# Last pair of experts: both first matrices fetched and multiplied ahead of both second matrices, and the last half matrix fetched in three parts

## The reference

```python
def reference(x, ...):                       # x (1, 256, 1024), all float32
    h = rmsnorm(x, mix_norm)
    z = h @ w_in                             # split: pool, q, k, v, indexer, gates
    y_pool = pool_mixer(z_pool) @ w_branch_pool
    y_attn = dsa_attention(q, k, v, ...) @ w_branch_attn
    x = x + (gates[0] * y_pool + gates[1] * y_attn) @ w_out
    h2 = rmsnorm(x, ffn_norm)
    x = x + moe(h2, ...)
    return rmsnorm(x, final_norm)

def moe(h, ...):                             # 256 tokens, 32 experts, 4 of them per token
    logits = h @ w_router + b_router
    top_vals, top_idx = top_k(logits, 4)
    gates = softmax(top_vals)
    combine = sum over the 4 of one_hot(top_idx) * gates
    for e in range(32):
        gu = h @ w1[e] + b1[e]               # w1[e] is 1024 x 2048: 8 MB
        g_ = min(gu[:, :1024], 7)
        u_ = clip(gu[:, 1024:], -7, 7)
        act = g_ * sigmoid(1.702 * g_) * (u_ + 1)
        out += combine[:, e] * (act @ w2[e] + b2[e])   # w2[e] is 1024 x 1024: 4 MB
```

## Time and profile before

| | |
|---|---|
| median of 3 runs | 1103.54 us (1103.14 to 1104.28) |
| the profiled execution | 1103.12 us |
| its span in the trace | 1101.2 us, so 1.9 us lie around it |
| PE busy | 1021.2 us, 93% |
| DVE, ACT busy | 28%, 20% |
| mean granted TensorE clock | 0.986 |
| moved | 438.34 MB, mean 398 GB/s |

### The profile page before, as it was taken

How to read it: one execution, slowest core, us unless ns; L and a number is a source line. 1 busy time by engine, 2 the same in 40 slices (tenths; PEclk the granted TensorE clock), 3 DMA queues, 4 the chain that set the end, 5 groups by cost and what they waited for, 6 DMA issues and landing times.

```text
span 1101.2 us, 12231 instructions
## 1 busy us (share of the span) xinstructions
PE 1021.2 (93%) x4994; PEld 503.4 (46%) x4994; DVE 303.5 (28%) x689; ACT 218.6 (20%) x373; POOL 18.3 (2%) x26
## 2 busy tenths in 40 slices
PE   5999999999999999998998989898989898999896
PEld 5987776434343434343434343434333343434342
DVE  5866576221212121212121211212121111121212
ACT  6456644111111111111111101011101111111112
POOL 1100020000000000000000000000000000000000
PEclk9999999999999999999999999999999999999999
DMA  8784469999999999999999999999999999999994
GB/s 321 290 329 148 153 258 417 426 430 430 431 431 428 436 432 430 437 430 432 432 438 431 432 432 438 431 432 432 438 431 432 432 438 431 432 427 430 432 428 183
DMA packets 25635, 438.34 MB, mean 398 GB/s; under 512 B 3016, under 2 KB 3200, under 8 KB 5120
## 3 DMA queue, kind: packets, MB, share of 16 engines
q1 hardware_dynamic: 24432, 432.84, 92.5%
q0 software_dynamic: 1168, 5.01, 1.2%
HBM read 436.78 MB, written 2.11 MB: 399 GB/s over the span
## 4 chain that ended last, share of the span: by engine, by line
PE 67%; DMA 27%; DVE 2%; issue 1%; ACT 1%; SPq 0%; DVEq 0%; ACTq 0%
PE bank L1424 28%; DMA quad<-in_w 21%; PE bank L1473 14%; DMA place<-in_w 6%; PE bank L1085 6%; PE bank L1086 5%; PE bank L1087 5%; PE bank L1329 3%; PE bank L1286 1%; PE bank L1454 1%; DMA cst<-in_consts 1%; PE bank L1397 1%; PE bank L1379 1%; PE bank L1433 0%; DVE wl L712 0%
## 5 line engine op out<-in xcount | busy, mean ns | idle before, releaser
L1424 PE MATMUL bank<-quad,r 128*64 128x512 f32 x1280 | 294.4, 618 | 22.2 <-DMA quad<-in_w 22.2
L1424 PEld LDWEIGHTS bank<-quad,r 128*64 128x64 f32 x1280 | 98.3, 142 | 205.9 <-issue 201.5
L1424 PE MATMUL bank<-place,r 128*64 128x512 f32 x704 | 154.6, 595 | 4.8 <-DMA place<-in_w 3.7
L1473 PE MATMUL bank<-quad,r 128*64 128x512 f32 x640 | 141.7, 595 | 11.2 <-issue 7.8
L996 DVE TENSOR_SCALAR r<-bank 128x512 f32<-128x512 f32 x32 | 22.1, 692 | 404.9 <-PE bank L1424 391.9
L1018 DVE TENSOR_TENSOR ysl<-bank,ysh 64x512 fp32r<-64x512 f32 x62 | 42.7, 688 | 291.1 <-ACT ysh L662 290.1
L643 ACT ACTIVATE r<-r 128x512 f32<-128x512 f32 x32 | 20.2, 632 | 471.0 <-DVE r L996 471.0
L1424 PEld LDWEIGHTS bank<-place,r 128*64 128x64 f32 x704 | 49.4, 137 | 102.4 <-issue 94.9
L1473 PEld LDWEIGHTS bank<-quad,r 128*64 128x64 f32 x640 | 51.1, 137 | 90.5 <-issue 90.5
L1473 PE MATMUL bank<-place,r 128*64 128x512 f32 x352 | 78.0, 595 | 6.0 <-issue 5.3
L662 ACT ACTIVATE ysh<-bank 64x512 fp32r<-64x512 f32 x62 | 36.6, 591 | 225.6 <-PE bank L1473 224.8
(11 more groups left out here) (214 smaller groups left out, 815.4 us busy)
## 6 DMA issues: line engine op xcount, KB each, us to landing
quad<-in_w SPq DMA_DIRECT2D x60, 4096.0 KB, 29.3
place<-in_w SPq DMA_DIRECT2D x69, 2048.0 KB, 17.7
ring<-in_w_front SPq DMA_DIRECT2D x24, 1024.0 KB, 4.9
place<-in_w SPq DMA_DIRECT2D x2, 1024.0 KB, 34.7
place<-in_w_last SPq DMA_DIRECT2D x1, 2048.0 KB, 36.0
place<-in_w_last SPq DMA_DIRECT2D x2, 1024.0 KB, 34.7
ring<-in_w_idx SPq DMA_DIRECT2D x2, 768.0 KB, 6.8
xs<-in_x SPq DMA_DIRECT2D x2, 512.0 KB, 8.2
```

Of the source, the lines that this page charges most:

```text
L1424: ins = mm(bk[part, :], xgT[i // 2 % 2][:, k, own], w[:, c1:c1 + HALF], start=False, stop=k == KD - 1)
L1473: ins = mm(YT[part, :], a_k, w[:, kk, c1:c1 + HALF], start=k == 0, stop=k == KD - 1)
```

## The change

- The transfers of the last pair are issued in another order: chunks 12 to 15 w1 of 30, 16 to 19 w1 of 31, 20 and 21 w2 of 30, 22 and 23 w2 of 31. The places and the waits before each issue are the same. Chunk 21 is one transfer instead of two; chunk 23 is three (1 MB, 0.5 MB, 0.5 MB) instead of two.
- PE follows: w1 of 30, scatter of the former pair, gate transposes, transposes of `act` of 30 (now in bank `GATHER`, copied to a new tile `actT_even`), both biases, w1 of 31, w2 of 30 (in `YT`), transposes of `act` of 31, `scatter_even`, w2 of 31 (summed in `UA` and `GATHER`), with the scatter of the first half (`scatter_last(0)`) placed after half of the matmuls of the second.
- The gather that stood in expert 30 for an expert that doesn't exist is moved into the branch for experts with more than 64 tokens.
- ACT and DVE do their work for the last pair in that order.

The three functions `last_pair` below are, in this order, those of ACT, DVE and PE.

```diff
+            last_order = [(NE - 4, range(CHUNKS)), (NE - 3, range(CHUNKS)), (NE - 2, range(4)), (NE - 1, range(4)),
+                          (NE - 2, range(4, CHUNKS)), (NE - 1, range(4, CHUNKS))]
+            for c, (e, j) in enumerate((e, j) for e, js in last_order for j in js):
+                i = halves[c % (2 * QUADS)][0]
                 former = 2 * (c - 2 * QUADS + 1) if c >= 2 * QUADS else 4 * (c // 2 - QUADS + 1)
                 sp.wait_ge(chunks_used, (NE - GROUP) * STEPS + former)
+                if (e, j) == (NE - 1, CHUNKS - 2):
+                    sp.dma_start(place[i], w2_last[0, :, :]).then_inc(chunk_loaded[i], 16)
+                elif (e, j) == (NE - 1, CHUNKS - 1):
+                    for lo_col, hi_col, loaded in ((0, SLOT, chunk_loaded[i]), (SLOT, SLOT + PIECE, tail_loaded[0]),
+                                                   (SLOT + PIECE, CHUNK, tail_loaded[1])):
+                        sp.dma_start(place[i][:, lo_col:hi_col], w2_last[1, :, lo_col:hi_col]).then_inc(loaded, 16)
...
+            def last_pair():
+                u = NE - 2
+                sigmoid(u)
...
+                gates_transposed(PAIRS - 1)
+                act_transposed(u, actT_even, GATHER)
+                sigmoid(u + 1)
+                sums_high(last_used + KD + STEPS, slice(0, SLOTS))
+                act_transposed(u + 1, actT, GA)
...
+            def last_pair():
+                u = NE - 2
+                gate_picks(0, u)
+                activated(u, last_used + KD, u)
+                gates_low(PAIRS - 1)
+                activated(u + 1, last_used + 2 * KD, u + 1)
+                sums_low(u, slice(0, SLOTS))
+                for c, bk in enumerate((UA, GATHER)):
+                    v.wait_ge(chunks_used, last_used + KD + STEPS + 2 * (c + 1))
+                    nc.vector.tensor_copy(yl[c], bk[:, :]).then_inc(y_low, 1)
...
+            def last_pair():
...
+                pe.wait_ge(xgT_ready, 2 * PAIRS)
+                first_matrix(lo, c0)
+                scatter(u)
...
+                transposed_act(GATHER)
+                pe.wait_ge(sel_ready, u + 2)
+                bias1(UA, bu)
+                bias1(GA, bg)
+                first_matrix(hi, c0 + 4)
...
+                for c in range(2):
+                    w = last_chunk(c0 + 8 + c).rearrange("p (k n) -> p k n", k=4)
+                    for kk in range(4):
+                        k = 4 * c + kk
+                        for part, c1 in ((lo, 0), (hi, HALF)):
+                            ins = mm(YT[part, :], columns_of(actT_even, k), w[:, kk, c1:c1 + HALF], start=k == 0, stop=k == KD - 1)
+                        if kk % 2:
+                            ins.then_inc(chunks_used, 1)
+                pe.wait_ge(act_ready, u + 2)
+                transposed_act(GA)
+                scatter_even(u + 1)
+                pe.wait_ge(actT_ready, u + 2)
...
+                for c, bk in enumerate((UA, GATHER)):
+                    w = last_chunk(c0 + 10 + c).rearrange("p (k n) -> p k n", k=KD)
+                    for k in range(0, KD, 2):
+                        if c and k == KD // 2:
+                            scatter_last(0)
+                        if c and k >= KD // 2:
+                            pe.wait_ge(tail_loaded[(k - KD // 2) // 2], 16)
+                        for part, kk in ((lo, k), (hi, k + 1)):
+                            ins = mm(bk[part, :], columns_of(actT, kk), w[:, kk, :], start=k == 0, stop=k == KD - 2)
+                        if k % 4:
+                            ins.then_inc(chunks_used, 1)
+                scatter_last(1)
```

More of the change, by code:

```diff
@@ new lines, in sigmoid, with gates_transposed, act_transposed @@
+            def sigmoid(u):
+                a.wait_ge(gclip_ready, u + 1)
+                nc.scalar.activation(act, gclip, ACT.Sigmoid, scale=ALPHA).then_inc(sig_ready, 1)
+            def gates_transposed(pair):
+                a.wait_ge(gT_done, pair + 1)
+                nc.scalar.activation(gTh, YT[:, 0:SEQ], ACT.Copy).then_inc(gT_ready, 1)
+            def act_transposed(u, t, bk):
+                a.wait_ge(actT_done, u + 1)
+                nc.scalar.activation(t, bk[:, :], ACT.Copy).then_inc(actT_ready, 1)
@@ new lines, in sums_high, with expert_group @@
+            def sums_high(steps, own):
+                a.wait_ge(chunks_used, steps)
+                for c in range(2):
+                    nc.scalar.activation(ysh[own, c, :], YT[c * SLOTS:(c + 1) * SLOTS, :], ACT.Copy)\
+                        .then_inc(y_high, 1)
+            def expert_group(r, g, experts=GROUP):
+                for i in range(experts):
+                    u = r * NE + g * GROUP + i
+                    sigmoid(u)
+                    if i % 2 == 0:
+                        gates_transposed(r * PAIRS + g * (GROUP // 2) + i // 2)
+                    copy_xgT(r * (2 * PAIRS + 2) + g * GROUP + i + 3, i % 2, (i // 2 + 1) % 2)
+                    act_transposed(u, actT, GA)
+                    sums_high(u * STEPS + STEPS, slice((i % 2) * SLOTS, (i % 2 + 1) * SLOTS))
@@ L983, in expert_group @@
                     if i % 2 == 0:
[L985 to L1000, removed]
@@ L1015, in expert_group @@
[L1015 to L1019, removed]
+                        gate_picks(r, e)
+                    activated(u, u * STEPS + KD, e)
+                    if i % 2 == 0:
+                        gates_low(r * PAIRS + g * (GROUP // 2) + i // 2)
@@ new lines, in last_chunk, with transposed_act, columns_of @@
+            def last_chunk(c):
+                n, loads, _ = halves[c % (2 * QUADS)]
+                pe.wait_ge(chunk_loaded[n], 16 * (loads + 1 + c // (2 * QUADS)))
+                return place[n]
+            def transposed_act(bk):
+                for c in range(4):
+                    ins = nc.tensor.transpose(bk[:, c * P:(c + 1) * P], act[:, c * P:(c + 1) * P], ident)
+                ins.then_inc(actT_done, 1)
+            def columns_of(t, k):
+                return t[:, (k % 4) * P + (k // 4) * SLOTS:(k % 4) * P + (k // 4 + 1) * SLOTS]
@@ L1410, in expert @@
                 opening = isinstance(g, int) and g == 0
-                final = isinstance(g, int) and g == GROUPS - 1
                 late = isinstance(r, int)
@@ L1442, in expert @@
                     ins.then_inc(gT_done, 1)
-                    if final and i == GROUP - 2:
-                        for b in range(TB):
-                            ins = nc.tensor.transpose(YT[lo, SEQ + b * P:SEQ + (b + 1) * P], gpick[:, b, hi], ident)
-                        ins.then_inc(gT2_done, 1)
                     pe.wait_ge(pick_ready, r * (PAIRS + 1) + pair + 2)
@@ L1490, in _ @@
                     expert(0, g, i)
-            for i in range(GROUP - 1):
+            for i in range(GROUP - 2):
                 expert(0, GROUPS - 1, i)
-            last_expert()
+            last_pair()
             pe.wait_ge(count_ready, 1)
@@ L1496, in _ @@
             with pe.If(most > SLOTS):
+                pe.wait_ge(pick_ready, PAIRS + 1)
+                gather(0)
                 pe.wait_ge(xgT_ready, 2 * PAIRS + 1)
```

141 lines of the change are left out of this document (66 added, 75 removed).

## The result

| | before | after |
|---|---|---|
| median of 6 runs | 1103.1 us (1102.44 to 1104.28) | 1110.26 us (1106.95 to 1111.51) |
| ratio, 95% interval | | 1.0057 (1.0042 to 1.0072) |
| profiled execution, span | 1103.12, 1101.2 | 1111.51, 1109.7 |
| mean granted TensorE clock | 0.986 | 0.983 |

Slower, as forecast, but by 7.2 us of medians where 3.0 were forecast, and outside the range (1103.9 to 1107.9). The six executions fall in two groups: 1106.95 and 1107.43 (clock 0.985, 0.986), and 1110.22 to 1111.51 (0.983). The profiled one is of the second group.

A forecast was written before the change was run, and what follows sets the result against it. The prediction took PE's work behind chunk 21 to bound the tail, not the weight stream. Its terms summed to 20.27 us against 17.25, 3.0 us more: 1106.1 us for the profiled execution, 1106.5 for the median, range 1103.9 to 1107.9.

The forecast's parts named there:

- What bounds the tail: End of the kernel: PE's work behind chunk 21 sets the end, not the stream; last scatter starts 3.9 us after the last byte.
- The middle of the pair: Between w1 of 30 and the end of w1 of 31: costs nothing; w1 of 31 ends 1.2 us before chunk 20.
- The sum of the tail: From the landing of chunk 21 to the end of the scatter: 20.27 us against 17.25, 3.0 us more.
- second chunk of w2 of 30: Tail, after chunk 21 lands: PE waits for the chunk, then 16 rows take 3.65 us.
- uncovered sum: Tail, between w2 of 30 and scatter_even: ACT's ysh and DVE's ysl stand uncovered, 2.10 us.
- w2 and half of the scatter: Tail, after scatter_even: w2 of 31 with half of the last scatter put in, 8.92 us.
- copy: Tail, before the last half of the scatter: DVE's copy of the second half is uncovered, 0.77 us.
- last half of the scatter: Very end of the tail: the other half of the scatter takes 1.83 us.
- a scatter from rest: Last scatter starting from rest instead of out of a running stream: -0.1 to +0.2 us, taken as 0.
- the rival of the clock: PE's new wait before scatter_even lets the clock fall, slowing scatter_even and w2: +4.9 us, 1108.5; chance 0.05.
- The banks: Between w2 of 30 and scatter_even: full wait of 2.1 us kept despite different banks; with the rule about 1.5 us less.
- The cut in three: Chunk 23's transfers: last parts wanted some 6 us after the last landing, so the cut neither costs nor gives.

The follow-up runs named there:

- b_hide: Changed kernel with scatter_even between the halves of w2 of 31 and transposes of act of 31 ahead of the last chunk of w2 of 30: 1106.41 us.
- g_both: Changed kernel with scatter_even between the halves of w2 of 31 and the last scatter whole at the end, its copy covered: 1104.86 us, ratio 1.0013.
- h_half: Kernel before, with ACT's copy of the transposed act of 31 in two halves, w2 starting after the first: 1102.62 us, ratio 0.9996.
- a_fill: Changed kernel with one unread matmul in each of four PE waits: three for transfers, one before scatter_even: 1106.99 us, ratio 1.0039.
- Experiment 2: Changed kernel with the unread matmul only before scatter_even (1107.19 us), or only in the three waits for transfers (median of all six 1110.58 us).
- k_rest_fill: Kernel before, with scatter_even of 31 behind the transposes and two unread matmuls in PE's rest: 1105.94 us over 11 runs.
- c_late: Changed kernel with its end undone: last chunk in two halves, both halves of the last scatter after all of w2: 1107.93 us.
- f_fill_dma: Changed kernel with unread matmuls only in the three waits for transfers, none before scatter_even: median of all six 1110.58 us.
- j_rest: Kernel before, with scatter_even of 31 moved behind the transposes, so PE rests while DVE makes act: 1108.84 us, ratio 1.0052.
- e_fill_last: Changed kernel with one unread matmul only in the wait before scatter_even: 1107.19 us.
- i_fine: Kernel before, with ACT's copy in halves, the gather moved, finer w1 of 31 pieces, last w2 chunk whole: 1102.88 us, ratio 0.9996.
- d_order: Kernel before, with the gather moved, finer w1 of 31 pieces and three matmuls of scatter_even after the transposes: 1102.55 us, ratio 1.0004.

## Why the prediction was wrong, step by step

- **What bounds the tail** was right: work on PE behind chunk 21, not the stream. Nothing waited for chunk 23 in the changed kernel, and taking waits out of that work (b_hide, g_both) gave back what was forecast to within 0.6 us. The 0.3 us that h_half saved in its profile are too little to be seen in the medians.
- **The middle of the pair costs nothing**: right. w1 of 31 starts at 1056.62 instead of 1054.1, and still waits 1.01 us for its last chunk.
- **The sum of the tail**: forecast 20.27 us from chunk 21's release of PE to the last matmul; measured 23.95 (1077.87 to the start of the last square, 1101.82). Term by term, forecast and measured: second chunk of w2 of 30 3.65, 3.68; uncovered sum 2.10, 2.10; `scatter_even` 3.00, 4.20; w2 and half of the scatter 8.92, 11.18; copy 0.77, 0.77; last half of the scatter 1.83, 2.02.
- Of the 3.7 us too little, 3.3 is the clock: `scatter_even` +1.2, 24 rows of w2 7.38 for 5.32. Where the clock held (a_fill), the same two were 3.03 and 5.30. The other 0.4 is what I had put at nothing: two changes between w2 and scatter (0.08 and 0.12) and a scatter from rest (0.19).
- **The failed step** is the sentence in the rival of the clock: "PE waits for the stream in the same way all through the last experts, and the granted clock of those stages is 1.00". What it says of those stages is so (1.00 from 933 to 1094 us), but the new rest is not like those waits. In the kernel before they are 1.3 us at most, with 3.65 us of matmuls between them; the new one is 1.54 us, and with it PE has nothing but four transposes to do in 2.1 us. Experiment 2 parts the two. Which of these differences counts isn't shown. So the mechanism was there, but its chance, 0.05, was off: by their times four of six executions fell, and the median is of those. Its price was off as well: 1.9 us, taken from 3.8 us of slow PE at the kernel's start, while here the lower clock lasted 6.8 and cost 3.3.
- **The trace of before would have told more.** Its mean clock is 0.986, so it did fall somewhere, and I looked at the end only. The Trainium skill, page "TensorE: Matmul & The Clock Gate", section "HAM oscillation — how this bites in real kernels", has waits for transfers between bursts as the cause of such falls; I set it aside with "the waits of this trace don't bear that out". That reading was wrong: the kernel before falls eight times, each time at a wait of 2.6 to 2.7 us for a transfer of 4 MB (last section). The runs don't bear the rule out for the waits of 1.0 to 1.3 us, and the fall that cost time here came at a wait for VectorE.
- **The banks**: the full 2.10 us stood between w2 of 30 and `scatter_even`, as the written order had it and not as the rule of the Trainium skill, page "Perfetto Trace Analysis", section "Matmuls", would have had it: the banks differed, and the copies were still not covered. Once the order was changed (b_hide), 0.6 us of medians went against the held executions of a_fill, where 0.9 was forecast, and with it the clock's fall.
- **The rest of the distance.** Where the clock held, the changed kernel takes 1106.95 and 1107.43, and with the rest filled 1106.99 and 1107.19 (medians), against 1103.0 to 1103.1: 4.0 us. 3.0 + 0.4 of it is explained, and in a_fill's profile chunk 21 released PE at 1076.43, 0.3 after its landing before (1076.1). In the changed kernel's own profile it came 1.8 us later than before. Of that, 1.3 stand already in the middle of the kernel (PE starts at 524.25 where it started at 522.93), and the profiles of the six variants with the same code up to there have only 0.1 to 0.7. So most of it belongs to that one execution and not to the change.
- **The cut in three**: nothing waited for its parts, as forecast. No run takes it away alone.

## What to carry to other kernels

Before work is taken from TensorE or moved so that it waits, look for how long it rests there and what must still be done behind it: a rest of 1.5 us between transposes and `scatter_even` cost 3.3 us of clock here on top, twice its own length, in most executions, and one useless matmul in it gave them back. Count what must still be done once the transfer that bounds the tail is in; an order that hides one engine's chain but leaves more of TensorE's work behind that transfer loses. And if the mean granted clock is under 1.00, find where it fell and at which rest before giving a fall a chance of 5%.

## What the runs showed of the hardware

In the kernel before the clock falls too, eight times between 523 and 933 us, where PE waits for a transfer of 4 MB. One of them, timeline and stages:

```profile
919.84 7.09 PE L1424 MATMUL bank<-quad,r 128*64 128x512 f32 x32 [0.22 <-DMA quad<-in_w]
929.52 7.88 PE L1424 MATMUL bank<-quad,r 128*64 128x512 f32 x28 [2.59 <-DMA quad<-in_w]
```

```profile
926.00:929.50 3.50, 0.92 (x6) 0.05 (x3) 0.00 (x0) 0.00 (x0) 0.00 (x0) 1.00 0.95 412
929.50:932.90 3.40, 3.38 (x8) 1.10 (x10) 0.00 (x0) 0.00 (x0) 0.00 (x0) 0.50 1.07 463
932.90:936.00 3.10, 3.10 (x18) 1.15 (x16) 0.00 (x0) 0.00 (x0) 0.00 (x0) 1.00 1.03 444
```

PE rests 2.59 us, then runs at 0.50 for 3.4, and is back at 1.00. It costs nothing there, because PE would only wait longer for the next transfer: in the profile of k_rest_fill only the first of the eight falls is there, and from that first stage to the last (523.22 to 929.87) it takes 406.65 us, where the kernel before takes 406.59. Behind the stream the same kind of fall costs half its length, and it lasts longer: 6.8 us in all four profiles that have it (the changed kernel, c_late, f_fill_dma, j_rest), 3.4 in every fall under the stream. Why is not shown.

Neither the length of a rest nor what PE waits for tells alone whether the clock falls. Two waits for a transfer before the last chunk of w1 of 31, the first from g_both, the second from c_late:

```profile
1067.44 5.35 PE L1431 MATMUL bank<-place,r 128*64 128x512 f32 x16 [2.15 <-DMA place<-in_w]
```

```profile
1066.98 3.65 PE L1431 MATMUL bank<-place,r 128*64 128x512 f32 x16 [2.39 <-DMA place<-in_w]
```

In g_both the clock fell, and 16 rows took 5.35 us; the time was taken up by the waits for the next chunks. In c_late it held there, behind the longer wait. In the other profiles it held at waits for transfers of 1.92 (b_hide), 1.94 (k_rest_fill) and 2.17 us (e_fill_last), and fell at one of 1.95 (i_fine). The rest of 1.54 us before `scatter_even` let it fall in all three profiles that have it unfilled. The short matmuls of `scatter_even` without a rest before them don't: the kernel before, b_hide and g_both run them at 1.00.

The mean clock of an execution is a poor witness of all this: b_hide has 0.984 to 0.987 at nearly one time, and c_late has executions of 1107.74 with 0.983 and of 1107.93 with 0.996.

The other surprise is SP's queue: one transfer takes 0.33 us to issue, but in the profiles of d_order and i_fine, with more pieces of 0.5 and 1 MB ahead of them, the last issues took 4.1 to 5.9 us each. Two profiles show it; that it costs time in the other executions is not shown.
